# Hybrid pooling and windowed attention layer on eight cores: conversions spread over a later period, input requests ahead of transposes, gate blocks in halves

## What is computed

```python
h = modulate(rms_norm(x, norm_pre_g), shift, scale)        # shift, scale, gate from silu(c) @ w_mod + b_mod
xa, ga, q, k, v, gb, gm = split_columns(h @ w_in)
y_a = pool_mixer(xa, pool_w, pool_scale) * silu(ga)        # centred means of 2, 4, 8, 16 tokens minus the token
y_b = attend(q, k, v) * silu(gb)                           # +-128 tokens and all 256 context keys, 16 heads, 4 kv heads
g = sigmoid(gm)
merged = g[..., :D] * (y_a @ w_branch_a) + g[..., D:] * (y_b @ w_branch_b)
out = x + gate * rms_norm(merged @ w_out, norm_post_g)
```

## Time and profile before

| | |
|---|---|
| median of 3 runs | 2293.26 us (2290.36 to 2294.43) |
| profiled execution, its own time | 2304.11 us |
| span of its slowest core (core 1) | 2302.6 us (the cores: 2273.9 to 2302.6) |
| TensorE matmul busy | 2231.1 us, 97% |
| TensorE weight load | 1031.0 us, 45% |
| VectorE | 1276.3 us, 55% |
| ScalarE | 1191.8 us, 52% |
| GpSimd | 864.7 us, 38% |
| one exponential (128x512, L823, ScalarE) | 604 ns, x1264 |
| mean DMA rate | 156 GB/s |

### The profile page before, as it was taken

One profiled execution on the slowest core, in us unless ns is written; L12 is line 12 of the kernel. 1 busy time (PEld: TensorE's weight loads), 2 busy tenths in 40 slices (PEclk: granted clock), 3 DMA queues, 4 the chain that ended last, 5 costly groups with the idle time before them and its releaser, 6 DMA issues.

```text
span 2302.6 us, 50318 instructions; the slowest of 8 cores (2273.9 to 2302.6 us)
## 1 busy us (share of the span) xinstructions
PE 2231.1 (97%) x16392; PEld 1031.0 (45%) x16392; DVE 1276.3 (55%) x3172; ACT 1191.8 (52%) x2298; POOL 864.7 (38%) x1069
## 2 busy tenths in 40 slices
PE   7989899999999999999999999999999999999988
PEld 2434444444444444444444444444444444444443
DVE  1446555555645656565565656556565555656543
ACT  3654456554464555546455545645545565554532
POOL 1324343342433434343343434334343433434332
PEclk9999999999999999999999999999999999999999
DMA  9999756555465555647544564654556464554543
GB/s 264 210 145 163 184 141 157 155 143 147 138 170 165 140 140 143 178 133 168 173 137 144 156 171 132 172 166 128 141 152 166 137 163 148 145 138 147 138 161 119
DMA packets 209987, 358.12 MB, mean 156 GB/s; under 512 B 131900, under 2 KB 134076, under 8 KB 207432
## 3 DMA queue, kind: packets, MB, share of 16 engines
q1 hardware_dynamic: 206456, 337.02, 52.3%
q0 software_dynamic: 3280, 17.89, 6.0%
HBM read 305.89 MB, written 45.10 MB: 152 GB/s over the span
## 4 chain that ended last, share of the span: by engine, by line
PE 88%; DVE 3%; DMA 3%; issue 2%; ACT 1%; SPq 1%; POOL 1%; DVEq 0%; ACTq 0%; POOLq 0%
PE pb L628 38%; PE pb L929 9%; PE pb L1012 9%; PE pb L759 9%; PE pb L820 7%; PE pb L846 6%; PE pb L920 5%; PE pb L684 3%; PE pb L361 2%; DMA s_xt<-x 1%; DVE s_scr L645 1%; ACT s_PT L823 1%; DVE s_PT L833 1%; DMA s_ws<-wg_scr 1%; SPq L571 1%
## 5 line engine op out<-in xcount | busy, mean ns | idle before, releaser
L823 ACT ACTIVATE s_PT<-pb 128x512 bf16<-128x512 f32 x1264 | 651.8, 604 | 214.4 <-PE pb L820 214.2
L628 PE MATMUL pb<-s_hT,s_ws 128*128 128x512 bf16 x2720 | 642.5, 381 | 9.0 <-ACT s_Tm L895 5.5
L628 PEld LDWEIGHTS pb<-s_hT,s_ws 128*128 128x128 bf16 x2720 | 255.1, 98 | 337.1 <-issue 56.3
L963 POOL TENSOR_TENSOR s_mgT<-s_scr 128x512 bf16<-128x512 f32 x128 | 163.3, 1276 | 586.8 <-DVE s_scr L900 580.6
L628 PE MATMUL pb<-s_hT,s_W 128*128 128x512 bf16 x1600 | 369.0, 384 | 0.4 <-DVE s_yb L864 0.4
L900 DVE SCALAR_TENSOR_TENSOR s_scr<-s_Tm,pb 128x512 f32<-128x512 bf16 x256 | 175.3, 685 | 291.4 <-PE pb L929 121.5
L895 ACT ACTIVATE s_Tm<-pb 128x512 bf16<-128x512 f32 x256 | 154.9, 605 | 269.6 <-PE pb L628 219.0
L645 DVE TENSOR_TENSOR s_scr<-pb,s_ropet 128x512 f32<-128x512 f32 x320 | 204.5, 685 | 115.8 <-PE pb L628 91.7
L759 PE MATMUL pb<-s_W,s_hT 128*128 128x512 bf16 x1024 | 243.9, 381 | 0.7 <-DVE s_yb L864 0.7
L628 PEld LDWEIGHTS pb<-s_hT,s_W 128*128 128x128 bf16 x1600 | 151.6, 99 | 205.8 <-issue 42.3
L1012 PE MATMUL pb<-s_ws,s_mgT 128*128 128x512 bf16 x1024 | 238.5, 379 | 0.9 <-POOL s_mgT L963 0.9
(11 more groups left out here) (147 smaller groups left out, 2228.9 us busy)
## 6 DMA issues: line engine op xcount, KB each, us to landing
s_ws<-wg_scr SPq DMA_DIRECT2D x332, 512.0 KB, 4.5
s_xr<-x SPq DMA_DIRECT2D x62, 512.0 KB, 4.8
y<-s_xr SPq DMA_DIRECT2D x60, 512.0 KB, 5.0
s_xt<-x SPq DMA_DIRECT2D x57, 512.0 KB, 4.8
s_ropet<-rope SPq DMA_DIRECT2D x16, 512.0 KB, 4.7
wg_scr<-w_g POOLq DMA_DIRECT2D x16, 512.0 KB, 24.9
s_ws<-w_mod SPq DMA_DIRECT2D x5, 1024.0 KB, 14.8
s_PT<-x SPq DMA_DIRECT2D x9, 512.0 KB, 7.4
```

Of the source, the lines that this page charges most:

```text
L628: E("pe", lambda e, k=k, rhs=rhs: e.matmul(out=pb[:, :], lhsT=lhs(k), rhs=rhs, start=(k == 0), stop=(k == 7)), reads=hb + wbufs(k), writes ...
L823: E("act", lambda e, g=g: e.activation(out=PT[:, jb, g, :], in_=banks[g][0][:, :], func=AF.Exp, scale=0.125), reads=[banks[g][1]], writes= ...
L963: E("pool", lambda e: e.tensor_tensor(out=mgT[:, c, :], in0=u[0][:], in1=v[0][:], op=ALU.add), reads=[u[1], v[1]], writes=[bf(f"mgT{c}")])
```

## The change

Every edit is a matter of place and time in the queues; no compute instruction is added or removed.

1. `casts` holds ten blocks instead of sixteen. The six others (20, 14, 15, 16, 17, 21) are converted in the first period, at units 1, 6, 11, 16, 21 and 26.
2. `D2D0` goes from 26 to 35: first conversion, and the stores of two converted blocks.
3. `prep_scale` requests the next x tile 1.4 after the scaling, ahead of the transpose at 2.5.
4. Each gate block is emitted in two halves of cost 3.5, with attention steps possible between them; the sums follow 5.5 after the second half instead of 2.5 after the block.
5. The gating of the first four pool tiles comes 8, 8, 8 and 6.5 after the first sums, instead of 6, 6, 6 and 5. `load_gg` comes 8.0 after gate block 5, instead of behind the first q unit.
6. The residual rows of tile TT - 6 (58) have their place in `xt`, and are requested at unit 5 of the last period that has attention.

```diff
-        def mod_rows(blk, mid=None, keep=False):
-            pg, pgb = next_bank(keep)
+        def mod_rhs(blk, k):
+            if blk == 5 and k < 4:
+                return xr[k // 2][:, (k % 2) * 512:(k % 2) * 512 + 512], [bf(f"xr{k // 2}")]
+            t, bufs = STG[blk, k // 4]
+            return AP(t.tensor, t.offset + (k % 4) * 512, [list(t.ap[0]), [1, 512]]), bufs
...
-        def gate_rows(blk):
-            c0 = (blk - 4) * 512
-            later(2.5, P(gate_row_sums, blk, *mod_rows(blk, None, True)))
+        gbank = []
+
+        def gate_half(blk, h):
+            if h == 0:
+                gbank.append(next_bank(True))
+            pg, pgb = gbank[-1]
+            for k in range(4 * h, 4 * h + 4):
+                rhs, bufs = mod_rhs(blk, k)
+                E("pe", lambda e, k=k, rhs=rhs: e.matmul(out=pg[0:4, :], lhsT=fview(junk, k * 4, [[1, 4]]), rhs=rhs,
+                                                         start=(k == 0), stop=(k == 7)),
+                  reads=bufs + [bf("junk")], writes=[pgb], inc=(k in (1, 3, 7)))
+            if h:
+                later(5.5, P(gate_row_sums, blk, pg, pgb))
...
+            if t == TT - 6:
+                return xt[:], [bf("xt")], "d_rt"
             return xr[t % 2][:], [bf(f"xr{t % 2}")], f"d_r{t % 2}"
...
-            if t + 2 < TT - 4:
+            if t + 2 < TT - 4 and t + 2 != TT - 6:
                 later(4.0 if t % 4 < 2 else 24.0, P(load_res, t + 2))
 
-        OUT_LAG, D2D0, LEAD0 = 1.7, 26.0, 12.0
+        OUT_LAG, D2D0, LEAD0 = 1.7, 35.0, 12.0
...
             xs = norm_scale()
+            later(1.4, next_load)
             later(2.5, P(prep_turn, t, xs))
-            later(3.0, next_load)
...
+                if j == 1:
+                    for i, g_ in enumerate((20, 14, 15, 16, 17, 21)):
+                        ex.setdefault(1 + 5 * i, []).append(z(gcast, g_))
                 if not hasP:
-                    ex[5] = [z(gload, NLAST + i) for i in range(4)]
+                    ex[5] = [z(load_res, TT - 6)] + [z(gload, NLAST + i) for i in range(4)]
...
-        casts = list(range(4, 14)) + [20, 14, 15, 16, 17, 21]
+        casts = list(range(4, 14))
...
-        first += [(7.0, P(gate_rows, 4)), z(later, 3.0, first_slots)]
+        first += [(3.5, P(gate_half, 4, 0)), (3.5, P(gate_half, 4, 1)), z(later, 3.0, first_slots)]
         first += [(3.5, P(ctx_kv, 1))]
-        first += [(7.0, P(gate_rows, 5))]
-        first += [(3.46, P(q_unit, 1, 0)), z(load_gg, 0), z(pool_next, 2, 6.0), (3.46, P(q_unit, 1, 1)), (3.46, P(q_unit, 1, 2)), z(pool_next, 3, 5.0)]
+        first += [(3.5, P(gate_half, 5, 0)), (3.5, P(gate_half, 5, 1)), z(later, 8.0, P(load_gg, 0))]
+        first += [(3.46, P(q_unit, 1, 0)), z(pool_next, 2, 8.0), (3.46, P(q_unit, 1, 1)), (3.46, P(q_unit, 1, 2)), z(pool_next, 3, 6.5)]
```

12 lines of the change are left out of this document (5 added, 7 removed).

## The result

The changed kernel takes **2262.96 us** in the median of 3 runs (2261.09 to 2289.89), against 2293.26 us before. The ratio is 0.987 (0.9866, 95% interval 0.9838 to 0.9895), so it is 30.3 us faster in the medians; the 2289.89 us are of an execution in which cores 4 to 7 had a granted clock of 0.975 to 0.986, and the ratio leaves it out. The forecast was 2265 us with a range of 2256 to 2284: the time lies in it, 2 us from the forecast. But two terms of the sum were wrong, in opposite directions, as the traces and the experiments show. And the prediction also gave a figure for the profiled execution, 2276.0 us; there the change took off 41.2 us (2304.11 to 2262.96) and not 28.1.

What follows compares the result with a forecast made beforehand. TensorE, busy 97% of the span, was taken as the bound, with loss in the front (up to 250 us) and last 80 us. Terms summed to 28.1 us: median 2293.3 - 28.1 = 2265 us, range 2256 to 2284.

Steps and rivals of the forecast that it cites:

- first conversion, halves, bank, pool gating: Front: later conversion gains 5.7 us, half gate blocks with later sums 4.2, held bank costs 0.6, tile 2's pool gating gains 1.0.
- x tile of the first period: First period: x requested ahead of the transpose goes out about 10 us earlier, landing near 227 us; gain 6.0 us (0 to 6.9).
- request order in the steady part: Every fourth tile: earlier x request removes about 2.8 of ScalarE's 5 us wait and most TensorE waits; 5.0 us (0 to 6.6).
- residual rows: Last 80 us: tile TT-6's rows at hand in xt start VectorE's evacuation 5.4 us earlier; 6.8 us with the clock effect.
- moved conversions: First period: six conversions moved there from the front cost 0, landing soon enough that TensorE does not wait.
- the wait on xa: Near 121 us: TensorE's 4.0 us wait on ScalarE's xa evacuation goes, plus 1.7 us if the clock comes back.
- the mask: Near 146 us: TensorE's 3.2 us wait for tile 1's mask goes, as gate sum and pool gating come behind it.
- The bank held by gate block 5: Front, tile 2's last two score steps: one bank short until an exponential frees it; cost 0.6 us (0 to 1.2).
- Rival (a): Front's waits are taken over by others, as saturated DMA makes transfers no earlier; half the gain, 13 us, 2280; chance 0.19.
- (b): Rival, first period: converted blocks land late, SP held at the fetch delays v; priced at 20 us, 2285; chance 0.07.
- (d): Rival, steady part: transpose behind 512 KB of x lands up to 2.3 us too late per period; 2302, slower; chance 0.06.
- (c): Rival, whole kernel: no effect, since profiled waits lie off the slowest core's path in undisturbed runs; 2293; chance 0.05.

## Why the prediction was right, and where it was not

| term | predicted | shown |
|---|---|---|
| first conversion, halves, bank, pool gating | 10.3 | 11.1 (marks of four cores) |
| x tile of the first period | 6.0 | 0 net (80.7 us before and after); 3.3 for the request edit alone, 4.6 by leaving it out |
| request order in the steady part | 5.0 | 14.1 in the marks of four cores (1926.0 - 1911.9); 11.6 by leaving it out; 19.3 in time for the edit with all it does |
| residual rows | 6.8 | 5.5 in time; 5.7 by the marks of eight cores |
| moved conversions | 0 | no wait of SP on them; 1.9 us of TensorE's waits for weight blocks behind 300 us, on core 0 |
| sum | 28.1 | 30.3 |

**The front.** The mechanisms and sizes held: the wait on xa, the first conversion and the mask as the prediction has them. The bank held by gate block 5 shows as 0.6 us in the list, the value taken (`L832 <- ACT s_PT L835: 0.6`); from start to start the block takes 161.03 - 159.51 = 1.52 us, so 1.0 more than undisturbed, still within the bounds. The clock came back with the waits: 1.90 and 1.91 us for the blocks named. But this gain isn't the edits' own. Alone, the halves lost 5 us and the conversions gained nothing that the times show, since the first period took back all of the one gain and part of the other. With conversions, request and halves together it stayed (leaving out the halves: 7.3 us of front and 6.4 us of time lost).

**The first period.** The step that failed is the landing of the x tile. The prediction sent the request off at 218.7 us and had it land near 227, with ScalarE's wait under 3 us. The request went off at 222.13, behind three fetches that took 4.50 us to issue, and ScalarE had the tile 15.25 us later, not 7.8: it waited 12.95 us. The 7.8 us had been taken for the tile's own travel. The landings of SP's transfers show what they were. On core 0 of after the transpose of 213.43 us lands at 231.7, the three fetches at 233.4, 234.7 and 236.0, the x tile at 237.3 and the transpose behind it at 238.2. On core 1 of before the transpose of 218.73 us lands at 235.5, the x tile at 236.8, and the three fetches behind it at 238.1 to 241.2. In both they land in the order of their issue, 0.9 to 1.9 us apart. So the tile came when the line in front of it was through, and asking 7 us earlier, behind three fetches, didn't shorten that line. Rival (a) had this argument, and its counter-argument, that no wait of TensorE named a DMA in first place, was a poor one: the row of ScalarE behind the named link did name one. With conversions moved, residual loads moved, or both, one wait went and another came, and the period took 80.7 us or more. The request edit without the others does it in 77.4 us, but from a start 10.5 us later. So the 6.0 us of the term were there in part (3.3 alone, 4.6 among the others), and the earlier start of the period, which the other edits bring, took as much back. It is not shown what would lower the period from the early start.

**The steady part.** The mechanism was right and the size off by a factor of two to three. The step that failed is the price of a small wait: the prediction took the sum in the list of waits (6.6 us) as the upper end, where the nine blocks cost 15.1 us. The timeline beside it had this: six matmuls in 1.07 us, behind two in 0.50, where eight take 0.61. The likely value within the bounds was wrong, and so was the bound. The reading "so the loss sits in the front and in the last 80 us" came from two stretches that end at 300 us; half of the gain came from between. What was right is how much of ScalarE's own wait would go: about 2.8 of the 5 us, and at the place shown 4.95 us became 2.10.

**The tail.** 5.5 us in time (3 to 8), against 6.8. The traces say that the mechanism held, the clock too: in the mean of the eight cores the stretch from the last period's mark to the end takes 184.2 us before, 178.5 with this edit alone and 177.8 after, and 2.0 to 2.2 us of that lie behind the last transposes. The wait itself was 3.9 to 6.8 us by core and is 0.9 to 1.2. So it is 5.7 to 6.4 us by the marks, and the 6.07 us of the prediction are core 1's wait, where the mean of the eight is 4.7. The next wait was the one named.

**The rivals.** (b) and (d) didn't occur; (b) wasn't met in the moved conversions either, as told there. For (d), the landing of x tile transposes between 1000 and 1150 us, core 0 of after:

```profile
DMA to landing us min/median/max: 4.6/5.6/6.7
```

Against 3.1/5.9/6.5 the least is 1.5 us more and the most 0.2. These are four transposes each; over all of 300 to 2100 us on core 1 it is 3.1/3.9/8.4 before and 4.0/5.4/7.4 after. So the transpose does land later behind 512 KB of x, by 1.5 us in the median, but far from the 4.7 that the rival needs and within the 3 us of slack. The converting DMAs of after:

```profile
DMA to landing us min/median/max: 6.4/14.6/42.8
```

The Trainium skill's fit (DMA: Bandwidth & Descriptors, Anatomy of one DMA) gave 4.4 us, as an estimate; the least of these is 6.4 (before 8.6, not quite twice the 4.4), so the rows again speak against building on it. (c) falls by the ratio's interval.

So the time came out right by luck: two errors cancelled, 6.0 us too much in the first period and up to 1.3 in the tail, against some 7 to 9 us too little in the steady part (11.6 and 14.1 against 5.0). A third thing helped. The terms were read on the slowest core of an execution 10.9 us above the median, and the sum was carried over to the median unchanged. In the profiled executions the slowest core fell by 41.2 us and the mean of the eight by 32.2, so against its own base the sum was 13 us short. Before, the slowest core was the one with the most small waits, 25.5 us over 1741 (some 4 of them the 0.81 stretches of that execution), where core 4 lost 5. The edit makes all cores alike (1741 to 1742 us on seven of eight), so its worth is what the *slowest* core had lost to such waits.

## What to carry to other kernels

Price a small wait from the start of the block in front to the start of the block behind, and compare with the same pair undisturbed: here a wait listed at 0.8 us cost 1.8, and nine that sum to 6.6 us cost 15.1. Look at the same mark on all cores before pricing an edit: the scatter between cores that do the same work (20.5 us here, 1746.2 to 1766.7) was nearer to what the slowest core lost (25.5) than the list of waits was. Read the landings of a queue one by one before taking the time from a request to its landing for the transfer's own. In a stretch where the DMA engines are saturated, an earlier request moves the wait but not its end, and an edit that gains there alone can lose, or gain only once the others are in.

## What the hardware showed beyond this

- A block of eight matmuls of 32 rows that gets two of its PSUM banks late, one after the other, loses most of its rate: 0.55 us undisturbed, 2.34 us with one listed wait of 0.83 us, each instruction unchanged at 371 ns.
- Transfers that SP issued landed in the order of issue in the saturated stretch (before core 1, after core 0). When four conversions of 1 MB each went out within 18 us, fetches of 512 KB issued among them took 22.5 to 24.1 us to land, where 4.7 to 5.6 us are enough for three of them at 239 to 243 us of after.
- In the saturated stretch SP needs 11.11 us to issue one DMA transpose, 3.82 us another, and 1.22 us in the steady part; two plain requests took 6.89 us there, and 0.33 to 0.42 us is usual for one. The landings were late there too: 15.7 and 18.3 us for the first two transposes, 5.6 in the median of the earlier trace rows's stretch after.
- Two waits of 0.71 and 0.83 us within 2 us (ending at 535.99 and 537.32 us, before, core 1) were followed by eight matmuls in 3.15 us and a window of 2 us at 1.2 GHz (0.50). But two of 0.75 and 0.84 us (ending at 670.27 and 671.61 us, core 3) were followed by eight in the usual 1.90 us and a clock of 1.00. A single one of 0.83 us was followed by the usual 1.90 us at 1760.23 us of core 1, and by a clock of 0.50 behind 1875.86 us of core 7. The length of the waits doesn't tell which.
